# A hybrid encoder trunk on one core: the second layer's memory projection is put ahead of its output and query projections and takes the group norm's tiles among its units, and inverse roots are formed as exp(-ln/2) on ScalarE

## The reference, cut to what matters

```python
    state, y = lax.scan(_wkv7_step, state0.astype(f32), seq)
    ...
    mean = jnp.mean(y, axis=-1, keepdims=True)
    var = jnp.mean(jnp.square(y - mean), axis=-1, keepdims=True)
    o = ((y - mean) * lax.rsqrt(var + RW_GN_EPS)).reshape(B, L, D) * lnx_w.astype(f32) + lnx_b.astype(f32)
    ...
    o = (o + bonus.reshape(B, L, D)) * g.astype(f32)
    out = o.astype(h.dtype) @ w_o
...
def memory_cross_attention(h, mem_k, mem_v, w_q, w_o):
    q = (h @ w_q).reshape(B, L, XA_HEADS, XA_HEAD_DIM)
    ...
    for layer in range(DEPTH):
        ...
        h = rms_norm(x, p['norm_xattn'][layer])
        x = x + memory_cross_attention(h, mem_k[layer], mem_v[layer], p['xa_w_q'][layer], p['xa_w_o'][layer])
        h = rms_norm(x, p['norm_ffn'][layer])
        x = x + swiglu_ffn(h, p['ffn_w_gate_up'][layer], p['ffn_w_down'][layer])
    y = rms_norm(x, p['norm_final'])
```

## Time and profile before

| what | value |
|---|---|
| median of 3 runs (2394.7 to 2399.92 us) | 2396.86 us |
| the profiled execution | 2406.39 us, its span 2404.7 us |
| mean granted TensorE clock | 0.943 |
| busy share of the span, PE / DVE / ACT / POOL | 93% / 51% / 22% / 10% |

### The profile page before, as it was taken

The page is one execution under the profiler, slowest core; times in us unless marked ns, Lnnn a source line. Parts: engine busy times, 40 slices in busy tenths (PEclk is TensorE's granted clock), DMA queues, the critical chain, the costliest instruction groups (busy, mean ns, idle before and its releaser), DMA issues. The chain is left out here.

```text
span 2404.7 us, 49794 instructions
## 1 busy us (share of the span) xinstructions
PE 2232.0 (93%) x21876; PEld 2102.9 (87%) x21876; DVE 1235.1 (51%) x1658; ACT 525.0 (22%) x905; POOL 234.7 (10%) x289
## 2 busy tenths in 40 slices
PE   6997999998899999996999899988699899999997
PEld 5996777898599999995988899976599599999996
DVE  5434444654475555435657544431565376555434
ACT  2004445411321010000237222212311321101000
POOL 3001000100010000010000232210410110000010
PEclk9998888999899999997999999996899899999998
DMA  3222111236023222232121000001135123322221
GB/s 100 87 87 72 53 53 45 64 122 184 0 80 88 87 87 87 81 88 79 54 78 46 7 4 4 4 17 41 53 116 157 44 71 88 87 87 87 81 88 61
DMA packets 308560, 169.53 MB, mean 70 GB/s; under 512 B 10808, under 2 KB 304640, under 8 KB 308416
## 3 DMA queue, kind: packets, MB, share of 16 engines
q1 hardware_dynamic: 304784, 154.56, 22.2%
q10 hardware_dynamic: 3632, 12.81, 1.4%
HBM read 155.94 MB, written 11.41 MB: 70 GB/s over the span
## 5 line engine op out<-in xcount | busy, mean ns | idle before, releaser
L258 PE MATMUL psum<-words_r,weights_high_r 128*128 128x272 f32 (+1 forms) x7808 | 1492.4, 291 | 34.4 <-DVE weight_ring_r L209 22.6
L258 PEld LDWEIGHTS psum<-words_r,weights_high_r 128*128 128x128 f32 x7808 | 1234.2, 190 | 43.6 <-DVE weight_ring_r L209 35.1
L258 PE MATMUL psum<-words_r,weight_ring_r 128*128 128x272 f32 (+1 forms) x3904 | 1130.7, 290 | 0.0
L258 PEld LDWEIGHTS psum<-words_r,weight_ring_r 128*128 128x128 f32 x3904 | 740.0, 190 | 0.0
L204 DVE TENSOR_SCALAR weights_high_r<-weight_ring 128x1024 fp32r<-128x1024 f32 (+1 forms) x258 | 176.3, 683 | 511.1 <-PE psum L258 503.4
L209 DVE TENSOR_TENSOR weight_ring_r<-weight_ring,weights_high_r 128x1024 fp32r<-128x1024 f32 (+1 forms) x264 | 319.2, 1209 | 11.4 <-ACT weights_high_r L343 2.6
L399 POOL TENSOR_TENSOR words<-words,words 128x544 f32<-128x544 f32 x42 | 74.5, 1775 | 1062.1 <-ACT words L386 1062.1
L2105 PE MATMUL psum<-words 64*64 64x64 f32 (+1 forms) x3408 | 136.9, 229 | 0.5
L1439 ACT ACTIVATE words<-words 128x544 f32<-128x544 f32 x44 | 29.0, 659 | 452.7 <-DVE words L1383 452.7
L2105 PEld LDWEIGHTS psum<-words 64*64 64x64 f32 x3408 | 125.3, 135 | 1.8 <-DVE words L2028 1.8
L209 DVE TENSOR_TENSOR words_r<-words,words_r 128x544 fp32r<-128x544 f32 (+2 forms) x132 | 110.9, 858 | 27.5 <-ACT words_r L1007 16.7
(11 more groups left out here) (302 smaller groups left out, 2137.2 us busy)
## 6 DMA issues: line engine op xcount, KB each, us to landing
weight_ring<-in_ffn_w_gate_up_dram SPq DMA_DIRECT2D x88, 512.0 KB, 3.8
weight_ring<-in_xa_w_kv_dram SPq DMA_DIRECT2D x32, 512.0 KB, 3.9
weight_ring<-in_ffn_w_down_dram SPq DMA_DIRECT2D x32, 448.0 KB, 3.5
weight_ring<-in_sb_w_qkv_dram SPq DMA_DIRECT2D x24, 512.0 KB, 3.7
weight_ring<-in_xa_w_q_dram SPq DMA_DIRECT2D x16, 512.0 KB, 3.8
weight_ring<-in_xa_w_o_dram SPq DMA_DIRECT2D x16, 512.0 KB, 3.7
weight_ring<-in_ffn_w_down_dram SPq DMA_DIRECT2D x16, 512.0 KB, 3.7
weight_ring<-in_sb_w_o_dram SPq DMA_DIRECT2D x8, 512.0 KB, 3.7
```

Of the source, the lines that this page charges most:

```text
L258: last = nc.tensor.matmul(c.psum[0:job.m(u), 2 * q + h, 0:w], weights[:, k, :], x[:, k, h * w:(h + 1) * w], start=job.opens(u) and k == 0 ...
```

## The change

The second layer gets a stage of its own, `gate_and_query`, in place of the stages 1 to 4; `mix_and_query` stays for the first layer. In it the job order is `kv`, `o`, `xq`. The group norm becomes a class `GroupNorm` with one step per tile of 128 channels: PE subtracts the mean with a matrix `centre` (identity less 1/64 of the block of ones) into PSUM banks 4 and 5, ACT squares from there, PE sums each head into banks 6 and 7 with `head_ones`, ACT forms the inverse root as Ln and Exp, PE makes the gate into banks 2 and 3, DVE multiplies, weighs and adds, and gates, ACT and DVE make the high and low parts. Tile 0 is done ahead of the first unit of `kv`; tiles 1 to 7 stand among its units 0 to 13, and `kv` keeps to banks 0 and 1.

`Follow` and `Memory` form their inverse roots with Ln and Exp on ACT, with no DVE instruction; an ACT table set that holds both is loaded at five places ahead of them by `preload_act_table_set`. `wkv` no longer waits for its final stores: ACT waits for them later (`states_stored`). The buffers of the second layer are laid out anew (`mem_parts`, `xqs`, `kvs`, `kv_rows`, `s_rows`, the spaces of `wkv`), and two small constants are added (`eps`, `centre`).

```diff
@@ class Follow
     def take_root(self, act):
+        nc, c = self.c.nc, self.c
+        act.wait_ge(self.summed, 1)
+        nc.scalar.activation(self.root.rearrange("p (a b) -> p a b", a=2), c.psum[:, 6:8, 0:HALF], ACT.Ln, scale=1.0 / D,
+                             bias=c.eps[:, 0:1]).then_inc(self.meaned, 1)
         act.wait_ge(self.meaned, 1)
-        self.c.nc.scalar.activation(self.root, self.root, ACT.Sqrt).then_inc(self.rooted, 1)
-
-    def invert(self, dve):
-        dve.wait_ge(self.rooted, 1)
-        self.c.nc.vector.reciprocal(self.inv, self.root).then_inc(self.inverted, 1)
-        dve.wait_ge(self.inverted, 1)
+        nc.scalar.activation(self.inv, self.root, ACT.Exp, scale=-0.5).then_inc(self.inverted, 1)
@@ mix_and_query, scalar
             mem.load(act)
+            nc.scalar.preload_act_table_set("natural_log_exp_and_others")
             if split:
                 split.scalar(act)
@@ wkv, sync
-            sp.wait_ge(stored, 32)
@@ class GroupNorm
+    def square(self, act, p):
+        act.wait_ge(self.centred, p + 1)
...
+    def invert(self, act, p):
+        nc, inv = self.c.nc, self.inv[p % 2]
+        if p >= 2:
+            act.wait_ge(self.scaled, p - 1)
+        act.wait_ge(self.summed, p + 1)
...
+    def scale(self, dve, p):
+        nc, c, y = self.c.nc, self.c, self.y[:, p:p + 1, :]
+        dve.wait_ge(self.inverted, p + 1)
+        nc.vector.tensor_tensor(halves(y), c.psum[:, 4:6, 0:HALF], self.inv[p % 2].rearrange("p (a b) -> p a b", a=2), ALU.mult).then_inc(self.scaled, 1)
+        dve.wait_ge(self.scaled, p + 1)
+        dve.wait_ge(self.biased, p + 1)
...
+        dve.wait_ge(self.weighed, p + 1)
+        dve.wait_ge(self.gated, p + 1)
+        nc.vector.tensor_tensor(halves(self.parts.full[:, p:p + 1, :]), self.gate, halves(y), ALU.mult).then_inc(self.full, 1)
@@ gate_and_query
+            mem.load(sp)
+            gn.load(sp)
+            for u in range(RING):
+                load_unit(c, sp, kv, 0, u)
+            stream_weights(c, sp, kv, o)
+            stream_weights(c, sp, o, xq)
+            stream_weights(c, sp, xq, nxt)
...
+            def among(j):
+                p = 1 + j // 2
+
+                def run(n):
+                    if p < PAIRS and j % 2 == 0 and n == 2:
+                        pe.wait_ge(mem.low, KT)
+                        gn.sum(pe, p)
+                    if p < PAIRS and j % 2 == 0 and n == 5:
+                        gn.make_gate(pe, p)
+                    if p + 1 < PAIRS and j % 2 == 1 and n == 3:
+                        gn.centre(pe, p + 1)
+                return run
+
+            gn.centre(pe, 0)
+            gn.sum(pe, 0)
+            gn.make_gate(pe, 0)
+            gn.centre(pe, 1)
+            pe.wait_ge(gn.logged, 1)
+            for g in range(4):
+                mem.turn(pe, g)
+            for j in range(kv.per):
+                multiply_unit(c, pe, kv, 0, j, mem.low if j == 0 else None, among(j))
+            pe.wait_ge(gn.full, PAIRS)
+            pe.wait_ge(*out_of(c, kv, kv.per - 1))
+            for u in range(o.per):
+                multiply_unit(c, pe, o, 0, u, gn.low if u == 0 else None)
+                if 1 <= u <= 4:
+                    turn_rows(u - 1)
...
+            gn.scale(dve, 0)
+            split_unit(c, dve, kv, 0, 0)
+            for g in range(4):
+                mem.take_low(dve, g)
+            gn.take_low(dve, 0)
+            for j in range(kv.per):
+                if j + 1 < kv.per:
+                    split_unit(c, dve, kv, 0, j + 1)
+                p = 1 + j // 2
+                if p < PAIRS:
+                    if j % 2 == 0:
+                        gn.scale(dve, p)
+                    else:
+                        gn.take_low(dve, p)
...
+            gn.square(act, 0)
+            gn.bias(act, 0)
+            gn.invert(act, 0)
+            for p in range(1, PAIRS):
+                gn.bias(act, p)
+            mem.normalise(act)
+            gn.take_high(act, 0)
+            for g in range(4):
+                mem.take_high(act, g)
+            gn.square(act, 1)
+            act.wait_ge(states_stored, 32)
+            for j in range(kv.per):
+                p = 1 + j // 2
+                if j % 2 == 0 and p < PAIRS:
+                    gn.invert(act, p)
+                if j:
+                    keep(j - 1)
+                if j % 2 == 0 and p < PAIRS:
+                    gn.take_high(act, p)
+                if j % 2 == 1 and p + 1 < PAIRS:
+                    gn.square(act, p + 1)
```

More of the change, by code:

```diff
@@ L2313, in _ @@
+            for u in range(xq.per):
+                multiply_unit(c, pe, xq, 0, u, norm.low if u == 0 else None)
+                if u == 0:
+                    pe.wait_ge(rows_copied, 4 * MT)
+                    norm.tensor(pe)
+                if 3 <= u <= 6:
+                    turn_cached(u - 3)
+        @block.gpsimd
+        def _(pool):
+            norm.pool(pool)
         @block.vector
         def _(dve):
-            over(dve, "mean", "d", lambda it, g: nc.vector.scalar_tensor_tensor(
-                out=halves(y[:, bass.ds(it * 2 + g, 1), :]), in0=banks(g), scalar=-1.0 / HD,
-                in1=halves(y[:, bass.ds(it * 2 + g, 1), :]), op0=ALU.mult, op1=ALU.add))
@@ L2325, in _ @@
-            over(dve, "high", "low", lambda it, g: take_low(c, tile(out.low, it, g), tile(out.full, it, g), tile(out.high, it, g)))
+            gn.scale(dve, 0)
[10 more added lines that the diff above has]
+                        gn.scale(dve, p)
+                    else:
+                        gn.take_low(dve, p)
@@ new lines, in _ @@
+            split_unit(c, dve, o, 0, 0)
+            split_unit(c, dve, o, 0, 1)
+            for u in range(o.per):
+                norm.add(dve, u)
+                if u + AHEAD < o.per:
+                    split_unit(c, dve, o, 0, u + AHEAD)
+                else:
+                    split_unit(c, dve, xq, 0, u + AHEAD - o.per)
+                if u >= 1:
+                    norm.take_low(dve, u - 1)
+            norm.take_low(dve, KT - 1)
+            for u in range(xq.per):
+                dve.wait_ge(*done(c, xq, u))
+                if u + AHEAD < xq.per:
+                    split_unit(c, dve, xq, 0, u + AHEAD)
+                if u == 0:
+                    dve.wait_ge(norm.inverted, 1)
+                nc.vector.scalar_tensor_tensor(out=halves(q_out[:, u:u + 1, :]), in0=psum_of(c, xq, u), scalar=(D // XH) ** -0.5,
+                                               in1=norm.inverse(), op0=ALU.mult, op1=ALU.mult).then_inc(c.slot_emptied[xq.slot(u)], 1)
@@ L2335, in _, with keep @@
-            over(act, "full", "high", lambda it, g: nc.scalar.activation(tile(out.high, it, g), tile(out.full, it, g), ACT.Copy))
-        @block.gpsimd
-        def _(pool):
-            with pool.Fori(0, PAIRS // 2) as it:
-                for g in range(2):
-                    pool.wait_ge(s["n2"], it * 2 + (g + 1))
-                    nc.gpsimd.tensor_tensor(tile(y, it, g), tile(y, it, g), tile(bonus, it, g), ALU.add).then_inc(s["n3"], 1)
-                    pool.wait_ge(s["n3"], it * 2 + (g + 1))
-                    nc.gpsimd.tensor_tensor(tile(out.full, it, g), tile(y, it, g), tile(gate, it, g), ALU.mult).then_inc(s["full"], 1)
+            def keep(j):
+                act.wait_ge(*done(c, kv, j))
+                nc.scalar.copy(kv_out[:, j, :], psum_of(c, kv, j)).then_inc(c.slot_emptied[kv.slot(j)], 1)
@@ new lines, in _ @@
+            keep(kv.per - 1)
+            for k in range(KT):
+                norm.scalar(act, k)
+                if 1 <= k <= 4:
+                    copy_rows(k - 1)
+            act.wait_ge(rows_copied, 4 * MT)
+            for i, out in enumerate(("prompt_mem_k", "prompt_mem_v")):
+                act.dma_start(c.outs[out][layer, 0].rearrange("(m p) h d -> p m (h d)", p=P), kv_rows[:, :, i * D:(i + 1) * D]).then_inc(stored, 16)
+            norm.take_root(act)
+            for s in range(RING):
+                act.wait_ge(c.unit_done[s], xq.base)
```

268 lines of the change are left out of this document (145 added, 123 removed).

## The result

The changed kernel takes 2334.0 us (median of 4 runs, 2327.49 to 2335.99), the kernel before beside it 2398.39 (median of 4, 2394.7 to 2403.58): a ratio of 0.9714, with a 95% interval of 0.9697 to 0.9731. Measured once more, 5 runs against 9, it is 2334.09 and 0.9719 (0.9706 to 0.9733). The prediction said 2336. The profiled execution of after took 2327.49 us (span 2326.0, clock 0.966), the lowest of its four, while the profiled one of before, 2406.39, lies above all four of before here: the two spans differ by 78.7 us, the medians by 64.4.

What follows compares the result with a forecast made beforehand. TensorE, busy 93% of the span, bounds the kernel; 98.6 us without a full PE could be won. Section -53.1, tails -7.1, +0.5 and -1.1 make -60.8 us: 2336 us from 2396.86. Range 2325 to 2357, chance 0.8.

Steps and rivals of the forecast that it cites:

- (a): Transition from `wkv` to the new stage: 1.7 us for the barriers, without the 2.7 us wait for the states' store.
- (b): Start of the new stage, from the transition to the first matmul of `kv`: 22 us, bounds 18 to 30.
- (d): Group norm matmuls of seven tiles among the `kv` units: 24.5 us added, PE setting the pace at 9.4 us a pair.
- (f): Between `kv` and `o`, PE waits for the last copy out of PSUM: 0.7 us, bounds 0 to 1.5.
- (c): Same units of the three projections as before: 153.3 us, less 2.1 for memory transposes, plus 0.9 for row transposes: 152.1.
- (g): End of the section: one DVE step behind the last unit of `xq` and the barrier stay, 1.6 us.
- a tail's step: In the two tail norms, from PE's sum to the scaled output: 1.5 us instead of 5.07, saving 7.1 us for both.
- the freed barrier: End of the first feed-forward: one freeing of semaphores goes, with its second barrier, -1.1 us.
- first layer's table load: In the first layer's mix, the explicit table load delays the first high part: +0.5 us.
- the rival of paced pairs: DVE and ACT's chain, not PE, sets the pace of the `kv` pairs: 14 us more, 2350 us; chance 0.15.
- (e): First unit of `kv`: +1.1 us, 0.4 waiting for the last low part and 0.7 for the lower clock; bounds 0 to 6.
- The rival that feared the gate on 80 partitions: Clock drops within the pairs at the gate's instructions and units next to them: 13 to 33 us more, 2359 us; chance 0.10.

Runs made afterwards that it cites:

- The tiles ahead of the units: The changed kernel with group norm tiles 1 to 7 one behind the other ahead of the first unit of `kv`: 2357.28 us, ratio 0.9812.
- the passes added to DVE: The changed kernel with three more DVE passes over 544 columns in each of seven pairs of `kv` units: 2338.07 us in one run.
- roots alone: The kernel before with only the new Ln and Exp roots of `Follow` and `Memory` and their table loads: 2391.71 us, ratio 0.9960.
- stage alone: The changed kernel with the roots of `Follow` as before and no table loads in the feed-forward: 2339.56 us, ratio 0.9744.
- the reordered start: The changed kernel with late biases, second tile's centring between memory transposes, DVE and ACT steps reordered, first layer's table load later: 2333.31 us, ratio 0.9716.
- the two gate kernels: The kernel before with other operands in the gate's stage, on 128 partitions: 2386.13 us; on 80 partitions of the same tensors: 2399.21 us; one run each.
- the fed: fp32 matmuls thrown away where PE waits around the new stage's start: on the changed kernel 2333.08 us; fewer, with the start in another order, 2331.48 us.

## Why the prediction was right, point by point

| step of the prediction | predicted | after, profiled |
|---|---|---|
| (a) transition | 1.7 | 1.95 |
| (b) to the first unit | 22.0 | 19.84 |
| units of `kv` with the tiles, (d) to (f) | 72.8 | 72.57 |
| units of `o` and `xq`, the rest of (c) | 105.6 | 103.44 |
| (g) end | 1.6 | 1.33 |
| section | 203.7 | 199.13 |
| a tail's step | 1.5 | 1.47 |
| the freed barrier | -1.1 | -0.96 |
| first layer's table load | +0.5 | +0.46 |

The third row is 46.5 of units, 24.5 of tiles, 1.1 and 0.7; (c) less those 46.5 is the fourth. Of the signs that the prediction named, the first unit came after 19.8 us and not 22, the pairs take 9.41 us with the clock at 0.99, and the tails have no reciprocal left. The clock of 0.53 that the start shows is no sign against it, since the sum had put the start at the lower level.

**The pairs.** This term decided whether the change pays, and it was right: 9.41 us a pair where 9.4 was forecast, PE without a wait inside the pairs, the gate's eight instructions 2.00 us at the upper level. The tiles ahead of the units show what would have gone otherwise, and the passes added to DVE show that no chain paces the pairs; the rival of paced pairs falls with them.

**The start.** Three small terms were too long. PE was still at the upper level for the first centring (1.23 us, not 2.0; when the changed kernel was profiled again it took 2.15, and the first unit came at 20.8), and the biases and the memory's norm took 4.56 and 5.1 us where I had 4.9 and 5.6. The mechanism was as told: ACT's list, and once it is shortened, the landing of the gate's weights with PE at the lower clock. Two readings of PE's list were wrong and cost nothing here, because ACT's was longer: the gate's weights landed after 8.5 us, not 8 at the latest, and the second tile's centring (2.02 us) was left out. PE was free at 14.3 us and waited only 0.92 for the memory's norm.

**The units of `o`, and (e).** Of the 53.0 us of `o` before, at 0.94, the prediction took 5.6 as run at the lower level, half of which is lost. It left these 2.8 us in (c) and put only 0.7 more into (e), for the 7 us at the lower level that it expected at the first units of `kv`: 3.5 us lost in all. The trace shows less. The third of each three matmuls of 256 columns takes 0.41 us at 1618.90 and 0.28 at 1619.44, so the lower level ends some 1.6 us into the first unit and costs some 0.8 to 1.0, an estimate from these rows. This term was about 2.5 us too large, and its excess is booked in the fourth row, where `o` runs at 1.00 and `o` and `xq` take 2.2 us less than summed. That the third row agrees to 0.3 us owes something to this booking.

**The roots.** 3.6 us at each tail, none at the other four; roots alone and stage alone both bear it out. PE's sum ahead of it ran at either clock: in the last tail it took 2.18 us instead of 1.32, so that tail gained 2.7 net in this profile, and in the first 1.29 instead of 1.93, so that one gained 4.2. The Trainium skill, ScalarE: Activation LUTs, section "What ACT_TABLE_LOAD costs", adds a drain of 1380 ns to a load of 1283: in the trace the square begins 1.30 us behind the start of the load (1597.85 to 1599.15), so the load is there and the drain is not. In the reordered start the load begins 0.01 us behind an activation and the next one 1.30 us behind the load's start.

**The clock.** The rival that feared the gate on 80 partitions had its mechanism right and its place wrong: alone its matmuls stay at 0.50 (29.38 us), between units on 128 partitions they run at the upper level. The Trainium skill, TensorE: Matmul & The Clock Gate, section "Why this matters for your kernels", advises continuous work; the two gate kernels agree with it on 128 partitions and differ on 80.

**The sum.** -57.7 for the section, -7.2 for the tails, -0.96 and +0.46 make -65.4, where the prediction had -60.8; the medians give -64.4 and -65.6. That 2336 came within 2 us of 2334.0 has a share of luck: the kernel before was 1.5 us slower beside the changed one than in the runs that the prediction started from, and the section is 199.1 us in one profile of the changed kernel and 200.25 in the other. The profiled spans differ by 13 us more than the sum, nearly all in stages whose code the change leaves as it was. The largest such stretch is the first layer's attention, by the table of before, and of after:

```profile
185.00:411.00 226.00, 204.81 (x1125) 164.41 (x1126) 94.74 (x101) 110.91 (x134) 19.09 (x27) 0.86 0.20 58
```

```profile
185.00:406.10 221.10, 193.13 (x1126) 153.36 (x1126) 94.78 (x101) 110.25 (x134) 18.38 (x26) 0.92 0.21 58
```

It ends 4.9 us earlier (0.7 of which it had at its start) with as many instructions and a higher granted clock. This belongs to the execution, not to the kernel: the kernel with the roots alone, which has before's stages, passed the same store at 405.9 (before 411.0, after 406.1), the one with added passes of DVE, which has after's, at 410.9, and the fed and the reordered start read 0.86 in that stretch again.

The second such stretch is the first layer's cross attention with the start of the feed-forward, from POOL's first copy to the first sum of squares: 76.4 us in before and 72.0 in after, but 76.3 when the changed kernel was profiled again. The third, the stage between the first tail and `wkv`, is not settled. It takes 211.9 us in before and 208.9 in after; the four kernels with the old roots in the tails have 210.5 to 211.9, nine of the ten with the new ones 208.8 to 209.2, and the reordered start 210.4. Up to 3 us may thus be a gain of the roots that no term of the prediction has. No run shows its cause.

## What to carry to other kernels

A chain of short steps over independent tiles is worth taking out of its own stage when another projection stands ready that doesn't need it: half a unit of matmuls ahead of each wait hid seven chains for the price of their matmuls. Ask of the projection's input whether it depends on the chain at all; here the last of three didn't, and could stand first. Cost the start of a stage as a list for each engine with its DMA, and place each step by when its input comes; another order won 3.6 to 4.7 us here, which only the section shows.

## What the runs showed of the hardware that I had not expected

Of 64 fp32 matmuls issued without a gap, those on 80 partitions ran at 0.50 to the end (29.38 us), those on 128 partitions of the same tensors took 17.42. Eight of the gate's matmuls on 80 partitions took 2.00 us among work on 128 partitions, and 3.99 at the start of the new stage.

Thrown-away matmuls raised the clock over the start from 0.53 to 0.91 and won nothing by themselves, since they were in the way at two places (1.4 and 1.8 us).

A stage with the same code, the first layer's attention, read a granted clock of 0.86 in four of the fourteen profiles and 0.90 to 0.93 in the others. It took 224.3 to 225.8 us in those four, 218.9 to 224.1 in the others. A gain of 4.7 us in a section was not to be told from the medians of five runs.
